# Two transformer blocks on one core: the gather for the next pair of experts between gate and up

## The reference

```
eid  = two experts of 32 per token (a group of 8, then the best two in it)
for each expert e:   x_e = the tokens that chose e
    y_e = (silu(x_e @ w_gate[e]) * (x_e @ w_up[e])) @ w_down[e]
y[token] = sum over its two experts of weight * y_e[token]
```

## Time and profile before

| what | value |
|---|---|
| median of 3 runs | 3254.17 us (3254.1 to 3257.19) |
| the profiled execution | 3253.54 us, its span in the profile 3251.7 us |
| mean granted clock of TensorE | 0.877 of full speed |
| PE / DVE / ACT / POOL busy | 74% / 20% / 12% / 5% of the span |
| moved by DMA | 724.52 MB, mean 223 GB/s |

### The profile page before, as it was taken

How to read it: one execution, slowest core, us unless ns; L and a number is a source line. 1 busy time by engine, 2 the same in 40 slices (tenths; PEclk the granted TensorE clock), 3 DMA queues, 4 the chain that set the end, 5 groups by cost and what they waited for, 6 DMA issues and landing times. The chain is left out here.

```text
span 3251.7 us, 35260 instructions
## 1 busy us (share of the span) xinstructions
PE 2408.4 (74%) x14449; PEld 1305.7 (40%) x14449; DVE 663.0 (20%) x1421; ACT 390.9 (12%) x599; POOL 152.2 (5%) x160
## 2 busy tenths in 40 slices
PE   7999465449898883596546888782539799734998
PEld 3333352334344341232323333231315577531776
DVE  2000233530000003201742000002343200265000
ACT  0000121221111110000412111110004000000000
POOL 0000000120000001000011000001010000000000
PEclk9999767669999997798877999996769899876999
DMA  7788401149999995576026999995320344411442
GB/s 258 295 304 294 134 1 33 41 182 399 423 423 423 423 422 198 199 288 239 1 73 277 423 423 423 423 422 204 122 77 23 114 155 154 139 65 58 130 153 80
DMA packets 179363, 724.52 MB, mean 223 GB/s; under 512 B 14501, under 2 KB 72742, under 8 KB 113489
## 3 DMA queue, kind: packets, MB, share of 16 engines
q1 hardware_dynamic: 164816, 676.24, 53.9%
q0 software_dynamic: 8672, 25.83, 2.7%
q10 hardware_dynamic: 5792, 21.32, 1.7%
HBM read 697.99 MB, written 23.25 MB: 222 GB/s over the span
## 5 line engine op out<-in xcount | busy, mean ns | idle before, releaser
L1481 PE MATMUL bank<-ring,arena 128*64 128x512 f32 x1632 | 376.7, 611 | 70.1 <-DMA ring<-moe_w_up 50.2
L431 PE MATMUL bank<-ring,actT 128*128 128x512 f32 x768 | 346.9, 605 | 26.5 <-DMA ring<-c_w_qkv 25.2
L530 PE MATMUL bank<-misc,arena 128*128 128x128 f32 (+1 forms) x390 | 73.2, 364 | 378.4 <-PEq L1710 130.5
L1893 PE MATMUL bank<-actT,ring 128*128 128x256 f32 x1408 | 309.0, 381 | 2.2 <-PEq L498 2.2
L1893 PEld LDWEIGHTS bank<-actT,ring 128*128 128x128 f32 x1408 | 268.6, 191 | 47.4 <-issue 11.5
L1270 PE MATMUL bank<-arena 128*64 128x512 f32 x1088 | 241.0, 595 | 23.4 <-ACT arena L1330 23.4
L1481 PEld LDWEIGHTS bank<-ring,arena 128*64 128x64 f32 x1632 | 115.6, 140 | 325.9 <-issue 218.8
L431 PEld LDWEIGHTS bank<-ring,actT 128*128 128x128 f32 x768 | 143.7, 192 | 229.1 <-issue 229.1
L530 PEld LDWEIGHTS bank<-misc,arena 128*128 128x128 f32 (+1 forms) x390 | 64.4, 191 | 392.4 <-issue 264.6
L1368 DVE TENSOR_TENSOR arena<-arena,bank 128x512 f32<-128x512 f32 x34 | 36.7, 1080 | 830.8 <-ACT arena L1328 830.8
L1470 PE MATMUL bank<-arena 128*128 128x64 bf16 x5280 | 165.3, 195 | 50.2 <-DVE arena L1360 50.2
(11 more groups left out here) (284 smaller groups left out, 1833.4 us busy)
## 6 DMA issues: line engine op xcount, KB each, us to landing
ring<-moe_w_gate SPq DMA_DIRECT2D x136, 1024.0 KB, 24.0
arena<-moe_w_down SPq DMA_DIRECT2D x136, 1024.0 KB, 21.6
ring<-ada_w SPq DMA_DIRECT2D x96, 1024.0 KB, 7.3
ring<-moe_w_up SPq DMA_DIRECT2D x68, 1024.0 KB, 24.0
actT<-moe_w_up SPq DMA_DIRECT2D x68, 1024.0 KB, 24.7
ring<-ffn_w SPq DMA_DIRECT2D x66, 1024.0 KB, 5.3
made_scratch<-arena ACTq DMA_DIRECT2D x34, 512.0 KB, 7.7
ring<-ab_w_in SPq DMA_DIRECT2D x14, 1024.0 KB, 7.9
```

The source lines that it names most:

```text
L431: mm = nc.tensor.matmul(self.bank[g % 6][:, :], lhsT(m, k), halves[k // 4][:, k % 4, :], start=(k == 0), stop=(k == KT - 1))
L530: mm = nc.tensor.transpose(self.bank[n][0:bw, q * P:(q + 1) * P], src(t)[:, k * bw:(k + 1) * bw], self.ident)
L1481: return self.nc.tensor.matmul(self.bank[j // 2][64 * i:64 * i + 64, :], xs[:, S * kt:S * kt + S], piece[:, k * DE:(k + 1) * DE], start=(k ...
L1893: mm = nc.tensor.matmul(bank[2 * (j % 2) + which][:, f * SEQ:(f + 1) * SEQ], w[:, k, f * P:(f + 1) * P], self.actT[:, k * T:k * T + SEQ], ...
```

## The change

The order of TensorE's work within a pair changes: the wait for `picked` and the gather for the next pair go from behind the fourth step to a place between the second and the third, so between gate and up. ScalarE's silu waits for two steps of the pair instead of four, and VectorE's product gets a wait of its own for the fourth step. What is computed, the transfers and the buffers are the same.

```diff
                 def pair(p, first, arrived):
                     pe.wait_ge(sc["tokens"], p + (first + 1))
                     for j in range(4):
+                        if j == 2:
+                            pe.wait_ge(sc["picked"], p + (first + 2))
+                            gather_pair()
                         arrived(p, 2 * j)
                         arrived(p, 2 * j + 1)
                         for k in range(4):
                             for i in range(2):
                                 mm = self.gateup_tile(i, j, k, slot(2 * j + 1 - i), A(XS + 512 * i, 512))
                         mm.then_inc(sc["used"], 1)
-                    pe.wait_ge(sc["picked"], p + (first + 2))
-                    gather_pair()
                     pe.wait_ge(sc["hidden"], p + (first + 1))
...
                 def pair(p, first):
-                    act.wait_ge(sc["used"], p * 6 + (6 * first + 4))
+                    act.wait_ge(sc["used"], p * 6 + (6 * first + 2))
                     nc.scalar.activation(A(SG, 512), bank[0][:, :], ACT.Silu).then_inc(sc["silu"], 1)
...
                     dve.wait_ge(sc["silu"], p + (first + 1))
+                    dve.wait_ge(sc["used"], p * 6 + (6 * first + 4))
                     V_.tensor_tensor(self.by_rows(A(HH, 512)), A(SG, 512).rearrange("p (j q f) -> p j q f", q=P, f=2),
```

## The result

The changed kernel takes 3263.26 us (median of 14 runs) against 3256.03 us (median of 14 runs of the kernel before, taken beside it). The ratio is 1.0023, with a 95% interval of 1.0015 to 1.0032: about 7 us slower, a small loss that the interval keeps clear of no change. One of the 14 executions on either side was far longer than the rest (4809 and 8331 us) and is left out of the ratio. The forecast was +4.6 us, which it counted as the same.

What follows compares the result with a forecast made beforehand. The prediction took the stream of weights to bound the loops, at 31.0 us a pair. Starts and ends summed +8.6 - 2.9 + 0.3 - 1.4 = +4.6 us on 3253.54, giving 3258.1 (median 3258.8), range 3255 to 3263.

Steps and rivals of the forecast that it cites:

- a steady pair that differs from 31.0 us: Steady pairs of the loops: a sign that the forecast is wrong, as they should stay at 31.0 us at 423 GB/s.
- 29.0 us a pair: TensorE's own chain in a layer 0 pair, without waits for weights: 29.0 us against 27.8 before, under the stream's 31.0.
- The term of +8.6 us: Start of layer 0: the wait for picks delays the up reloads, stream dry 14.9 us instead of 6.3; bounds +6.9 and +12.5.
- the down reload flowing by 743.8: First pair of layer 0: the down reload follows the up reloads, which last to 744.3, in time.
- the bare product at 1.2 us under a cover of 2.1: Every layer 0 pair: TensorE idles 1.2 us for the product, covered by its 2.1 us wait for weights.
- a rival with a chance of 0.03: Clock falls behind the new waits, 1.7 us twice a pair: layer 0 pairs +1.4 us, +25 us, 3284; chance 0.03.
- Forecast -2.9 us: End of layer 0: last pair's chain hangs on the second gate weights, down starts 2.9 us earlier; bounds 0 and -4.1.
- Forecast -1.1 us: Layer 1: start +0.3 us from a stream dry for 0.35, end -1.4 from an earlier last down.
- The faster one: Loops: waits for up weights are late issues, not bandwidth, and the gather fills them: 3180 to 3237 us; chance 0.04.
- The one in which the ends give nothing back: Layer ends: late gate weights bring no gain, starts cost 8.6 + 0.3: 3263.1, up to 3267 us; chance 0.12.
- The one of 41 us from the bare product: Loops become TensorE's, the product's 1.2 us paid in all 34 pairs: +41 us, with the start +50, 3304; chance 0.03.
- the weighing: Later up reloads: only one finding the queue empty pays; all 34 paid in full would make over 100 us.

Runs made afterwards that it cites:

- no_gather: The kernel before with the loops' gathers cut to two matmuls each, so it does not compute the result: 3250.23 us, ratio 0.9982 to before.
- gap_filled: The changed kernel with seven transposes of the identity into an unused bank behind the up steps: 3261.93 us, ratio 1.0027 to before.
- early_picks: The changed kernel with VectorE making the second pair's picks ahead of its loop over the extra blocks: 3247.12 us, ratio 0.9983 to before.
- first_pair_old: The changed kernel with the first pair of each layer in the old order on TensorE: 3251.71 us, ratio 0.9993 to before.
- early_filled: The changed kernel with the edits of both early_picks and gap_filled: 3248.63 us, ratio 0.9983 to before.
- layer1_only: The changed kernel with layer 0's gather put back behind the fourth step: 3254.85 us, ratio 1.0002 to before.
- late_silu: The changed kernel with silu waiting for all four steps again, as in the kernel before: 3274.11 us, ratio 1.0057 to before.

## Why the prediction was right, and where it missed

**The sum.** The median of 3263.26 us stands at the upper edge of the forecast's own range of 3255 to 3263, in a session in which the kernel before stood 1.9 us above the median that the forecast was built on. In the layers the traces show +8.25 and +0.5, so +8.75 us against +4.6. The 4.15 us between them are, by the paragraphs below, 0.1 at the start of layer 0, 1.7 in two further dry stretches behind it, 0.7 at its end, 1.6 in layer 1, and rounding. All lie on the same side, so the near hit doesn't come from errors that cancel, but the whole time shows some 1.5 us less than the layers, in code that did not change, and that is luck.

**What bounds the loops.** Right as a floor: the stream is full at 423 GB/s in every variant, and no_gather keeps the 31.0 us. Wrong as a picture of layer 0 after the change, by a sign that the prediction itself gave (a steady pair that differs from 31.0 us): I had TensorE at 29.0 us a pair, waiting for weights. It gains 1.8 us on the stream in the pairs of 29.2 and next to nothing in those of 30.9. In gap_filled it took seven pairs of 29.2 us, 13 us of gain, until it waited for weights; the changed kernel gains some 11 us in all of layer 0, and so it never comes to wait.

**The start of layer 0.** The term of +8.6 us was right to 0.1: 15.0 us of dry stream against 6.3, 8.7. early_picks and first_pair_old show that this wait is the loss. What I missed stands one line further: I had the down reload flowing by 743.8, in time for a stream that is full to 744.3. The down steps began when forecast but ran at 1.2 GHz at first, the reload was issued at 743.60, and another 1.3 us of the stream were missing. The clock is not all of it: in gap_filled the down reload was issued 9.6 us behind the first up reload instead of 11.3, and 0.9 us were missing still. What the rest hangs on was not traced.

**The clock.** This is the step whose mechanism failed, though it is not the largest term of the miss. The prediction costed the bare product at 1.2 us under a cover of 2.1, and put the clock in a rival with a chance of 0.03. In 11 of the 17 distances between pairs of layer 0 the down steps took 8.78 us, 1.7 us more. gap_filled fills the 1.14 us wait, and none does: the clock fell because of that gap. The rival had the right mechanism, but its price of 25 us was far off, since one fall a pair (30.9 us) still fits under the stream's 31.0. What it cost is 1.5 us of layer 0 by gap_filled and 1.2 by early_filled, each from one pair of traces.

The chance of 0.03 rested on one stretch of layer 1 in which the clock stood at 2.4 GHz. The same trace of the kernel before shows more. In layer 1 the third step of 13 pairs stands behind a wait of 2.5 us. In seven of them it took 3.65 us, but in six in a row, from 1861 to 2016 us, it took 5.2 to 5.35 us with the clock down to 0.50:

```profile
1861.27 5.35 PE L1481 MATMUL bank<-ring,arena 128*64 128x512 f32 x16 [2.50 <-DMA ring<-moe_w_up]
...
1863.00:1864.00 1.00, 1.00 (x6) 0.29 (x4) 0.00 (x0) 0.00 (x0) 0.00 (x0) 0.50 1.02 426
```

The step of 5.12 us behind 2.44 us in the earlier trace rows is another. So steady waits did bring the clock down before the change already. It cost nothing there, since the stream set those pairs.

**The end of layer 0.** Forecast -2.9 us. The last down step ends 10.1 us behind the stream before (1253.93 against 1243.8) and 7.9 behind it after (1261.56 against 1253.7): -2.2. The chain that I worked from the last gate weights never came into force, since the gate step did not wait for them; the down steps started by TensorE's own chain. The sum for layer 0 is then 8.7 + 1.3 + 0.4 - 2.2 = 8.2 of the 8.25 measured.

**Layer 1.** Forecast -1.1 us, measured +0.5 in the changed kernel and +0.2 in layer1_only. The missing bytes add up to 1.3 us more of stream than before, where I had 0.35. Some 0.7 of them lie at the start (microseconds 1766 to 1769), the rest in the microseconds 1776 to 1783, in which the stream moves 344 to 385 GB/s; no run traced it to a cause. The end gave 0.8 us back (the last down step ends 5.9 us behind the stream, 6.7 before), where I had 1.4.

**The rivals.** The faster one is refuted by no_gather: the waits were bandwidth. The one in which the ends give nothing back had the right size (+8.9) for a wrong reason; the ends gave 2.2 and 0.8 us back, and the further dry stretches took them, some of it through the fallen clock. The one of 41 us from the bare product fell with early_picks; late_silu shows how near it was, since 0.73 us more of gap was worth 11 us.

The page of the Trainium skill that speaks against a later reload ("DMA: Bandwidth & Descriptors", Rules for kernel authors) bears on the reloads that find the queue empty, as the weighing had it: of 34 the first of layer 0 (8.7 us), and by 0.7 us at most the first of layer 1. It was not paid in every pair: the time shows 7 us more, and not over 100.

## What to carry to other kernels

When a transfer stream sets a loop, cost a move of work at the two places where the stream is not behind a queue: the first reload after the start and the work behind the last bytes. Ask of each wait that you move what its releaser is doing in the first pass, not in the steady one; here VectorE's tables made a wait of 10.6 us of one that is zero in every later pair of layer 0, and a few lines on VectorE were worth more than the order on TensorE. And where a cover of 2 us is all that holds, count a fallen clock behind each new gap before you call the gap free, and look through the whole stage, not one stretch, for steps that already run slow behind the gaps of today.

## What the runs showed of the hardware

TensorE's clock fell to its lower level behind gaps of only 1.14 and 0.69 us with matmuls between and after them, in 11 of the 18 pairs of layer 0 and in 4 of the 16 of layer 1. With the 1.14 us filled by transposes no down step of either layer ran at the lower level. The length of the gap alone didn't decide: with 1.88 us in place of 1.14 (late_silu) the down steps of layer 0 were slow in 8 pairs and not in 11, and in the kernel before 13 waits of 2.5 us in layer 1 (2.47 to 2.54) were followed by a slow step six times.

In six of the twelve kernels (the changed one, early_picks, first_pair_old, gap_filled, late_silu and early_filled) TensorE also stood for 1.3 to 1.9 us inside a gather with nothing that released it, once per execution. It did so in the first of the extra pairs, but in first_pair_old in the second pair of layer 0, which is the first pass through the loop there. The cause stays open; no run tested it.
